# A fourth group of seven products in the down projection of the plain gated layers

## The chip, the cores and the metric

The kernel runs on one core of one Trainium2 chip. The metric is the device time of one execution in microseconds (us). Before the change the median of three runs was 2737.45 us (2737.21 to 2740.82).

## The reference

Two transformer blocks run one after the other on x of 512 tokens by 1024 channels, in float32. The first has two layers, each with a gated feed-forward network, a mixer (two kinds of attention and a short convolution), a second gated network and a gated per-token embedding. The second block has one layer: another mixer, a gated network with a convolution over tokens on its gate, and an embedding. The change is about the four plain gated networks of the first block:

```python
h = rmsnorm(x, g_pre)
x = x + 0.5 * rmsnorm((silu(h @ w_gate) * (h @ w_up)) @ w_down, g_post)
```

w_gate and w_up are 1024 by 2816, w_down is 2816 by 1024, which the kernel takes as 22 rows of 128 for the down product. The gated network of the second block has 24 such rows and keeps its old code.

## The kernel before

Five engines each run an instruction list of their own, written out by hand in the order of the source, and meet only at semaphores. Activations lie with channels on the 128 partitions and tokens along the free dimension. An engine that waits holds everything behind it in its list.

A float32 product is made of three matmuls in a reduced float32 format (`trio`, L742 to L744): high part of the weight times high part of the activation, low times high, high times low. So each piece of weight is split before use. `split_high` (L583) copies it on ScalarE into a rounded tile WH, `split_low` (L588) subtracts on VectorE and writes the rest to WL. The pieces are units of 128 by 1024 elements, and four pairs of tiles go round: the split of a unit waits until TensorE has finished the unit four before it. Activations have high and low parts too (HH, HL, and HIDH_HIGH, HIDL_LOW for the hidden rows).

Most products of a gated network are computed in groups of seven in place of eight (`tensor_seven`): a block is cut in quarters, sums of quarters of the weights are multiplied by sums of quarters of the activations, and the results are combined. A group has seven products (0 to 6), each of 24 matmuls of 256 columns. They accumulate in three banks of PSUM called x, y and z, and between them ScalarE copies partial results out: p1 after product 0, q5 after 1, u2 after 2, c11 after 3, u3 after 4, c21 after 6 (`scalar_copy`, L1697). Product 2 waits for p1, 4 for u2, 5 for q5, 6 for u3. VectorE makes c22 (L2542) and c12 (L2548) of them. Of the weight quarters, five are loaded by SyncE's queue; GpSimd's queue adds a further quarter onto two of them by an accumulating DMA (`gpsimd_weight_sums`, L3453), and VectorE adds two more times (`vector_weight_sum`, L2527, called weight sum 2 and 6 after the product that uses it). A quarter's buffer is free for the next load when the low part of the last product that reads it is done, or when weight sum 6 has read it. There are six such buffers.

A plain network has n = 11 blocks of gate and up columns: groups 0 and 1 done directly, groups 2 to 10 in sevens. Then comes the down projection, where the changed code stands:

- early rows (`tensor_early_rows`): rows 8 to 15 directly for one half of the output channels, four units of two rows, each of 24 matmuls of 512 columns;
- group 11 (g = n) and group 12 (n + 1): rows 0 to 7 in sevens, one half of the output each. They use sums of hidden rows, `row_sum` 0 to 3 (L2590), with a high part on ScalarE (L1753) and a low part on VectorE (L2615);
- group 13 (n + 2): rows 8 to 15 in sevens for the other half. Its row sums (`late_sum`) are made early, parked in device memory and fetched back (`sync_park`, `sync_fetch`) when group 12 has used the first ones;
- the last rows (`tensor_last_rows`): rows 16 to 21 directly into all eight banks. The four banks of one half get the result of group 11 by additions of VectorE (`vector_add`), the other four are seeded by ScalarE from the sums of groups 12 and 13 (`scalar_seed`, L1761), since their banks serve the groups until then.

The order around the change is written out in `scalar_ffn`, `scalar_early_rows`, `scalar_down_seven` for ScalarE and `vector_ffn`, `vector_early_rows`, `vector_first_down_seven` and so on for VectorE; `sync_sums` places the parked sums in SyncE's queue of loads.

## Time and profile before

| | |
|---|---|
| runs, median of three | 2737.45 us |
| profiled execution, its own time | 2738.5 us |
| its span, first to last instruction | 2736.6 us |
| TensorE matmul busy | 2727.2 us |
| VectorE, ScalarE, GpSimd busy | 2058.6, 1623.5, 142.1 us |
| granted TensorE clock | 1.00 of 2.4 GHz |
| read from device memory | 364.87 MB |

Times in the views are microseconds from the start of the span. Matmuls overlap, so the cost of one is the distance between successive starts and not its duration. The same holds for ScalarE and VectorE, where an instruction starts about 0.1 us before the end that the trace gives for the one ahead of it.

### The profile page before, as it was taken

What the parts mean: (1) busy time and instruction counts of PE and PEld (TensorE: products, weight loads), DVE (VectorE), ACT (ScalarE), POOL (GpSimd) and SP (SyncE); (2) the same over time, 40 slices, a digit from 0 to 9 for tenths busy, and PEclk for the clock granted to TensorE, in tenths of its full rate; (3) what the DMA queues carried; (4) which work ended last, traced back from release to release, by engine and by line L of the source; (5) the groups of instructions that cost most, each with busy time, mean ns of one, the idle gap of its engine ahead of it and who ended that gap; (6) DMA issues with size and microseconds to landing.
All of it is one profiled execution on the core that took longest, in us unless ns stands there. A gap on an engine that the chain in (4) does not pass through costs nothing.

```text
span 2736.6 us, 46133 instructions
## 1 busy us (share of the span) xinstructions
PE 2727.2 (100%) x18546; PEld 2488.6 (91%) x18546; DVE 2058.6 (75%) x2754; ACT 1623.5 (59%) x2519; POOL 142.1 (5%) x160
## 2 busy tenths in 40 slices
PE   9999999999999999999999999999999999999999
PEld 8999987599999999999976799999987889999998
DVE  7778766767687787787757587787876746989968
ACT  6556644665566685565626565566754546666665
POOL 0000000000000000000000000000001100000000
PEclk9999999999999999999999999999999999999999
DMA  7776614037776327775331247765233323777651
GB/s 220 180 196 174 178 55 101 17 101 185 190 211 162 103 84 206 178 213 158 93 92 49 93 131 178 207 164 169 78 97 92 93 77 101 181 194 203 153 179 55
DMA packets 177139, 382.55 MB, mean 140 GB/s; under 512 B 35616, under 2 KB 80032, under 8 KB 176928
## 3 DMA queue, kind: packets, MB, share of 16 engines
q1 hardware_dynamic: 159216, 315.63, 37.1%
q0 software_dynamic: 17568, 63.97, 13.7%
q8 instruction: 148, 2.42, 0.4%
q14 instruction: 63, 0.52, 0.1%
q10 hardware_dynamic: 144, 0.00, 0.0%
HBM read 364.87 MB, written 12.58 MB: 138 GB/s over the span
## 4 chain that ended last, share of the span: by engine, by line
PE 99%; DVE 0%; DMA 0%; issue 0%; ACT 0%; SPq 0%; DVEq 0%
PE banks L742 31%; PE banks L743 31%; PE banks L744 31%; PE banks L1292 1%; PE banks L1314 1%; PE banks L1351 1%; PE banks L1303 1%; PE banks L1355 0%; PE banks L1341 0%; PE banks L781 0%; PE banks L1445 0%; DVE PT L3179 0%; PE banks L1274 0%; PE banks L1238 0%; DMA X<-in_x 0%
## 5 line engine op out<-in xcount | busy, mean ns | idle before, releaser
L742 PE MATMUL banks<-HH,WH 128*128 128x256 f32 (+1 forms) x3244 | 1015.8, 313 | 0.6 <-DVE HL L2284 0.4
L743 PE MATMUL banks<-HH,WL 128*128 128x256 f32 (+1 forms) x3244 | 1010.9, 312 | 0.0
L744 PE MATMUL banks<-HL,WH 128*128 128x256 f32 (+1 forms) x3244 | 1010.7, 312 | 0.0
L742 PEld LDWEIGHTS banks<-HH,WH 128*128 128x128 f32 x3244 | 619.1, 191 | 43.6 <-issue 8.3
L743 PEld LDWEIGHTS banks<-HH,WL 128*128 128x128 f32 x3244 | 619.2, 191 | 34.7 <-issue 1.0
L744 PEld LDWEIGHTS banks<-HL,WH 128*128 128x128 f32 x3244 | 619.1, 191 | 34.1
L588 DVE TENSOR_TENSOR WL<-raw,WH 128x1024 fp32r<-128x1024 f32 (+1 forms) x308 | 370.5, 1205 | 215.6 <-ACT WH L583 214.4
L583 ACT ACTIVATE WH<-raw 128x1024 fp32r<-128x1024 f32 (+1 forms) x308 | 319.3, 1040 | 291.7 <-DVE raw L2527 121.9
L742 PE MATMUL banks<-SH,WH 128*128 128x256 f32 x1472 | 416.7, 283 | 0.8 <-issue 0.8
L743 PE MATMUL banks<-SH,WL 128*128 128x256 f32 x1472 | 416.6, 283 | 0.0
L744 PE MATMUL banks<-SL,WH 128*128 128x256 f32 x1472 | 416.6, 283 | 0.0
L588 DVE TENSOR_TENSOR WL<-extra_raw,WH 128x1024 fp32r<-128x1024 f32 x216 | 264.1, 1223 | 126.4 <-ACT WH L583 126.4
L583 ACT ACTIVATE WH<-extra_raw 128x1024 fp32r<-128x1024 f32 x216 | 227.3, 1052 | 133.1 <-DVE extra_raw L2527 95.8
L742 PE MATMUL banks<-HIDH_HIGH,WH 128*128 128x256 f32 (+1 forms) x936 | 293.1, 313 | 0.4 <-issue 0.4
L743 PE MATMUL banks<-HIDH_HIGH,WL 128*128 128x256 f32 (+1 forms) x936 | 292.1, 312 | 0.0
L744 PE MATMUL banks<-HIDL_LOW,WH 128*128 128x256 f32 (+1 forms) x936 | 292.0, 312 | 0.0
L742 PEld LDWEIGHTS banks<-SH,WH 128*128 128x128 f32 x1472 | 282.6, 192 | 1.2 <-issue 1.2
L743 PEld LDWEIGHTS banks<-SH,WL 128*128 128x128 f32 x1472 | 282.6, 192 | 0.0
L744 PEld LDWEIGHTS banks<-SL,WH 128*128 128x128 f32 x1472 | 282.6, 192 | 0.0
L588 DVE TENSOR_TENSOR WL<-spare_raw,WH 128x1024 fp32r<-128x1024 f32 (+2 forms) x141 | 170.6, 1210 | 73.4 <-ACT WH L583 72.8
L1697 ACT ACTIVATE C<-banks 128x512 f32<-128x512 f32 x224 | 132.5, 592 | 138.7 <-PE banks L744 136.4
L583 ACT ACTIVATE WH<-spare_raw 128x1024 fp32r<-128x1024 f32 (+2 forms) x141 | 146.1, 1036 | 94.5 <-PE banks L744 55.9
(341 smaller groups left out, 3666.8 us busy)
## 6 DMA issues: line engine op xcount, KB each, us to landing
extra_raw<-in_w_quarters SPq DMA_DIRECT2D x96, 512.0 KB, 4.3
raw<-in_w_quarters SPq DMA_DIRECT2D x48, 512.0 KB, 4.8
raw<-in_w_in SPq DMA_DIRECT2D x46, 512.0 KB, 3.7
spare_raw<-in_w_quarters SPq DMA_DIRECT2D x36, 512.0 KB, 4.1
extra_raw<-in_w_quarters POOLq DMA_DIRECT2D x36, 512.0 KB, 7.4
raw<-in_w_down SPq DMA_DIRECT2D x30, 512.0 KB, 3.7
extra_raw<-in_last_quarters SPq DMA_DIRECT2D x26, 512.0 KB, 4.3
raw<-in_w_quarters POOLq DMA_DIRECT2D x24, 512.0 KB, 6.0
```

What stands on the lines that cost most here:

```text
L583: e.activation(WH[tile_of[u]][:, 0:n], raw[raw_of(u)][:, 0:n], ACT.Copy).then_inc(*high.done((u,)))
L588: e.tensor_tensor(WL[tile_of[u]][:, 0:n], raw[raw_of(u)][:, 0:n], WH[tile_of[u]][:, 0:n].bitcast(F32), ALU.subtract).then_inc(*low.done((u,)))
L742: e.matmul(o, wh, ah, start=start, stop=False, skip_group_check=skip)
L743: e.matmul(o, wl, ah, start=False, stop=False, skip_group_check=skip)
L744: return e.matmul(o, wh, al, start=False, stop=stop, skip_group_check=skip)
L1292: e.matmul(ps[h][:, 0:w], QM[0:QK, 2 * q + h, i * P:w], KM[0:QK, 2 * q + h, 0:w], start=True, stop=False)
L1303: last = e.transpose(ps[2 + h][:, c], PB[t % 2 * 2 + h][:, c], ident)
L1314: last = e.matmul(target, vals[:, j, (head + h) * HD:(head + h + 1) * HD], source, start=j == 0, stop=j == TC - 1)
L1351: e.matmul(ps[4 + h][:, j * P:T], ntri, SP[:, h, j * P:T], start=False, stop=False, skip_group_check=True)
L1697: e.activation(target, third(bank), ACT.Copy).then_inc(*act.done((name, s, g)))
```

## The change

In the four plain networks (`four_down`), the early rows shrink from four units to one, rows 8 and 9. A fourth group, g = n + 3, takes rows 10 to 15 for the half that the early rows served, in seven products with three row pairs in place of four (`first = 1`), so of 18 matmuls each. It uses the same parked row sums as group 13 and weight quarters that were already laid out. The last rows begin with the seeded banks. ScalarE's and VectorE's lists are written anew for the stretch: high and low parts of rows 0 to 7 and of the row sums move further ahead or behind, those of rows 10 to 15 move into groups 11 to 13, and the seeds are interleaved with the fourth group's copies. The fetches of parked sums 2 and 3 move from the load of row 16 to loads of the fourth group's quarters.

```diff
+def four_down(s):
+    return s < 9
+def early_units(s):
+    return 1 if four_down(s) else 4
 def seven_groups(s):
-    return range(2, gated_groups(s) + 3)
+    return range(2, gated_groups(s) + 3 + four_down(s))
...
-                           *(((s, 11, "b11"), (s, 11, "b22")) if n > 11 else (W[s, "early", 0], W[s, "early", 2])))
+                           *(((s, 11, "b11"), (s, 11, "b22")) if n > 11 else (W[s, "early", 0], (s, 11, "sum"))))
...
-                if key == W[s, "down", DOWN_WHOLE]:
+                third, fourth = ((s, n + 3, "sum"), (s, n + 3, "b22")) if four_down(s) else (W[s, "down", DOWN_WHOLE],) * 2
+                if key == third:
                     sync_fetch(e, s, 2)
+                if key == fourth:
                     sync_fetch(e, s, 3)
...
-            late = g == gated_groups(s) + 2
+            late = g > gated_groups(s) + 1
+            first = 1 if g == gated_groups(s) + 3 else 0
...
-                    for kp in range(4):
+                    for kp in range(first, 4):
...
-                             early + late[2:] + late[:2], False)
+                             late + early if four_down(s) else early + late[2:] + late[:2], False)
...
-            for kp in range(4):
+            for kp in range(early_units(s)):
...
             if g == gated_groups(s) - 1:
-                return W[s, "early", i]
+                return W[s, "early", i] if i < early_units(s) else W[s, "seven", g + 1, i - 1]
...
                 if g == n - 1:
-                    scalar_hidden_high(e, s, 10)
-                    scalar_hidden_high(e, s, 11)
+                    for k in (0, 2) if four_down(s) else (10, 11):
+                        scalar_hidden_high(e, s, k)
...
+        def scalar_short_rows(e, s):
+            n = gated_groups(s)
+            scalar_c21(e, s, n - 1)
+            scalar_hidden_high(e, s, 4)
+            scalar_hidden_high(e, s, 6)
+            scalar_row_sum_high(e, s, 0)
+            split_high(e, W[s, "seven", n, 2])
+            scalar_row_sum_high(e, s, 1)
+            for k in range(1, DOWN_SEVEN, 2):
+                scalar_hidden_high(e, s, k)
...
+            if four_down(s) and g == n:
+                scalar_silu_half(e, s, n - 1, 1)
+                scalar_row_sum_high(e, s, 2)
             split_high(e, W[s, "seven", g, 4])
+            if four_down(s) and g == n:
+                scalar_row_sum_high(e, s, 3)
...
+            if four_down(s) and g == n:
+                for k in (10, 12, 14):
+                    scalar_hidden_high(e, s, k)
...
+        def scalar_last_down_seven(e, s, g):
+            x, y, z = seven_banks(s, g)
+            split_high(e, W[s, "seven", g, 3])
+            scalar_copy(e, s, g, "p1", 0, x, third(y), seven_free(s, g)[1][0])
+            split_high(e, W[s, "seven", g, 4])
+            scalar_seed(e, s, 0)
+            scalar_copy(e, s, g, "q5", 1, z, Q5C[:], vec.at("c22", s, g - 1))
+            split_high(e, W[s, "seven", g, 5])
+            scalar_copy(e, s, g, "u2", 2, x, place(s, g, 0, 1), vec.at("half_added", s, 0, 1))
+            split_high(e, W[s, "seven", g, 6])
+            scalar_copy(e, s, g, "c11", 3, y, place(s, g, 0, 0), act.at("seed", s, 0))
+            split_high(e, W[s, "down", DOWN_WHOLE])
+            scalar_hidden_high(e, s, DOWN_WHOLE)
+            scalar_copy(e, s, g, "u3", 4, x, place(s, g, 1, 1), vec.at("half_added", s, 1, 1))
+            scalar_seed(e, s, 1, act.at("c11", s, g))
+            split_high(e, W[s, "down", DOWN_WHOLE + 1])
+            scalar_seed(e, s, 2, vec.at("c12", s, g))
+            scalar_hidden_high(e, s, DOWN_WHOLE + 1)
+            scalar_copy(e, s, g, "c21", 6, x, place(s, g, 1, 0), act.at("seed", s, 1))
+            scalar_seed(e, s, 3, act.at("c21", s, g))
...
                 if g == n - 1:
                     vector_hidden_low(e, s, 8)
                     vector_hidden_low(e, s, 9)
+                    if four_down(s):
+                        vector_row_sum(e, s, 2)
                 split_low(e, after_seven(s, g, 1))
...
+        def vector_short_rows(e, s):
+            n = gated_groups(s)
+            vector_half_scale(e, s, n - 1, 1)
+            vector_weight_sum(e, s, n, 2)
+            vector_hidden_low(e, s, 4)
+            vector_hidden_low(e, s, 6)
+            split_low(e, W[s, "seven", n, 2])
+            vector_row_sum_low(e, s, 0)
+            vector_row_sum(e, s, 3)
+            vector_row_sum_low(e, s, 1)
+        def vector_first_of_four(e, s, g):
+            split_low(e, W[s, "seven", g, 3])
+            for k in range(1, DOWN_SEVEN, 2):
+                vector_hidden_low(e, s, k)
+            split_low(e, W[s, "seven", g, 4])
+            vector_half_hidden(e, s, g - 1, 1)
+            vector_row_sum_low(e, s, 2)
+            split_low(e, W[s, "seven", g, 5])
+            vector_row_sum_low(e, s, 3)
+            vector_weight_sum(e, s, g, 6)
+            split_low(e, W[s, "seven", g, 6])
...
+        def vector_third_of_four(e, s, g):
+            split_low(e, W[s, "seven", g, 3])
+            vector_hidden_low(e, s, 11)
+            vector_hidden_low(e, s, 13)
+            vector_hidden_low(e, s, 15)
+            split_low(e, W[s, "seven", g, 4])
+            vector_late_sum_low(e, s, 2)
+            split_low(e, W[s, "seven", g, 5])
+            vector_late_sum_low(e, s, 3)
+            vector_weight_sum(e, s, g, 6)
...
+        def vector_fourth_of_four(e, s, g):
+            vector_half_add(e, s, g - 1, 1, 0)
+            split_low(e, W[s, "seven", g, 3])
+            split_low(e, W[s, "seven", g, 4])
+            split_low(e, W[s, "seven", g, 5])
+            vector_weight_sum(e, s, g, 6)
+            split_low(e, W[s, "seven", g, 6])
+            split_low(e, W[s, "down", DOWN_WHOLE])
+            vector_hidden_low(e, s, DOWN_WHOLE)
+            vector_c22(e, s, g)
+            vector_add(e, s, g, 1, 1)
+            vector_c12(e, s, g)
+            vector_add(e, s, g, 0, 1)
+            vector_add(e, s, g, 0, 0)
+            split_low(e, W[s, "down", DOWN_WHOLE + 1])
+            vector_add(e, s, g, 1, 0)
+            vector_hidden_low(e, s, DOWN_WHOLE + 1)
```

## Rows read from the trace of the kernel before

**Rows 1.** The page: span, TensorE's busy time, granted clock in 40 slices.
```profile
span 2736.6 us, 46133 instructions
...
PE 2727.2 (100%) x18546; PEld 2488.6 (91%) x18546; DVE 2058.6 (75%) x2754; ACT 1623.5 (59%) x2519; POOL 142.1 (5%) x160
...
PEclk9999999999999999999999999999999999999999
```

**Rows 2.** Waits of TensorE: releaser, us in total, times, longest.
```profile
PE banks L742 <- issue: 1.2, 3, 0.6
```

**Rows 3.** Timeline of TensorE, first plain layer: start, duration, line, operation, tiles, shape.
```profile
231.82 0.40 PE L742 MATMUL banks<-HIDH_HIGH,WH 128*128 128x512 f32 x1
...
253.60 0.28 PE L742 MATMUL banks<-HIDH_HIGH,WH 128*128 128x256 f32 x1
...
273.76 0.28 PE L742 MATMUL banks<-HIDH_HIGH,WH 128*128 128x256 f32 x1
...
314.08 0.40 PE L742 MATMUL banks<-HIDH_HIGH,WH 128*128 128x512 f32 x1
```

**Rows 4.** VectorE's busy time, early rows to group 13: sum of four windows, one window.
```profile
253.58:273.74 20.16, 15.42 (x16) 1.00 0.48 131
...
sum 82.24, DVE 66.30; mean DVE 16.57
```

**Rows 5.** Timeline of VectorE in group 10, same layer.
```profile
220.34 1.22 DVE L2590 TENSOR_TENSOR HLF<-HLF,HIDF 128x1024 f32<-128x1024 f32 x1
221.47 1.22 DVE L2527 TENSOR_TENSOR extra_raw<-extra_raw,extra_raw 128x1024 f32<-128x1024 f32 x1
223.82 1.23 DVE L588 TENSOR_TENSOR WL<-extra_raw,WH 128x1024 fp32r<-128x1024 f32 x1 [1.12 <-ACT WH L583]
225.25 1.23 DVE L588 TENSOR_TENSOR WL<-raw,WH 128x1024 fp32r<-128x1024 f32 x1 [0.21 <-ACT WH L583]
226.40 1.29 DVE L2572 TENSOR_TENSOR HIDL_LOW<-HIDF,HIDH_HIGH 128x512 fp32r<-128x512 f32 x2
...
228.98 0.68 DVE L2542 TENSOR_TENSOR C<-Q5C,C 128x512 f32<-128x512 f32 x1
229.58 0.68 DVE L2548 TENSOR_TENSOR C<-banks,C 128x512 f32<-128x512 f32 x1
```

**Rows 6.** Timeline of ScalarE in group 10: split 6, c11, a split, u3.
```profile
222.73 1.06 ACT L583 ACTIVATE WH<-extra_raw 128x1024 fp32r<-128x1024 f32 x1 [0.59 <-DVE extra_raw L2527]
223.69 0.58 ACT L1697 ACTIVATE C<-banks 128x512 f32<-128x512 f32 x1
224.17 1.05 ACT L583 ACTIVATE WH<-raw 128x1024 fp32r<-128x1024 f32 x1
226.26 0.60 ACT L1697 ACTIVATE C<-banks 128x512 f32<-128x512 f32 x1 [1.04 <-PE banks L744]
```

**Rows 7.** DMA issues in the down groups: count, KB, median us to landing (last: one issue).
```profile
extra_raw<-in_w_down_quarters POOLq DMA_DIRECT2D x3, 512.0 KB, 5.4
raw<-in_w_down_quarters SPq DMA_DIRECT2D x5, 512.0 KB, 4.6
extra_raw<-in_w_down_quarters SPq DMA_DIRECT2D x4, 512.0 KB, 4.8
spare_raw<-in_w_down_quarters SPq DMA_DIRECT2D x3, 512.0 KB, 5.1
...
raw<-in_w_down_quarters POOLq DMA_DIRECT2D x1, 512.0 KB, 8.1
```

**Rows 8.** Timeline of the last layer's third down group: ScalarE, then TensorE.
```profile
2615.92 1.06 ACT L583 ACTIVATE WH<-extra_raw 128x1024 fp32r<-128x1024 f32 x1 [3.11 <-DMA extra_raw<-in_last_down_quarters]
...
2620.21 0.58 ACT L1697 ACTIVATE R<-banks 128x512 f32<-128x512 f32 x1
...
2620.55 0.28 PE L744 MATMUL banks<-HIDL_LOW,WH 128*128 128x256 f32 x1
2620.89 0.36 PE L742 MATMUL banks<-HH,WH 128*128 128x256 f32 x1
```

**Rows 9.** Timeline of ScalarE: the four seeds of the first plain layer.
```profile
314.56 2.16 ACT L1761 ACTIVATE banks<-C 128x512 f32<-128x512 f32 x4 [3.46 <-DVE C L2837]
```

More of the change, by code:

```diff
@@ L500, in place @@
         def place(s, g, t, m):
-            return two((R, RP)[t]) if g == gated_groups(s) + 2 else quadrant(t, m)
+            n = gated_groups(s)
+            if g < n + 2:
+                return quadrant(t, m)
+            return two((R, RP)[t]) if m else C[:, t, 0, :].rearrange("p (c t) -> p c t", c=2)
         def quarter_out(s, g, t, m):
@@ L561, in tiles_free @@
             if s is not None and STAGES[s] == "ffn":
-                e.wait_ge(*pe.at("unit", W[s, "seven", seven_groups(s)[-1 - (tile_of[u] == NSPLIT + 1)], 6]))
+                g = gated_groups(s) + 1 if tile_of[u] == NSPLIT + 1 else seven_groups(s)[-1]
+                e.wait_ge(*pe.at("unit", W[s, "seven", g, 6]))
             elif s is not None and STAGES[s] == "mix":
@@ L986, in seven_free @@
                 return group_free(s, g - 2 if g < n else n - 1)[:3]
-            first = [vec.at("evacuated", s, (n - 1) % 2, 3)] if g == n + 1 else [act.at("c21", s, n)]
-            return [first, [act.at("c11", s, g - 1)], [vec.at("c12", s, g - 1)]]
+            first = [vec.at("evacuated", s, (n - 1) % 2, 3)] if g == n + 1 else [act.at("c21", s, g - 2)]
+            second = [vec.at("half_added", s, 0, 0)] if g == n + 3 else [act.at("c11", s, g - 1)]
+            return [first, second, [vec.at("c12", s, g - 1)]]
         def row_sums(tile, i):
@@ L1033, in tensor_seven @@
                         last = trio(e, ps[bank][:, part(up)], high_of(u)[:, c], low_of(u)[:, c], *operand(kp),
-                                    opens and up == kp == 0, kp == 3, not (opens and up == 0))
+                                    opens and up == 0 and kp == first, kp == 3, not (opens and up == 0))
                 last.then_inc(*pe.done(("seven", s, g, ph), ("unit", u)))
@@ L1051, in tensor_ffn @@
             tensor_early_rows(e, s)
-            for g in seven_groups(s)[-3:]:
+            for g in down_groups(s):
                 tensor_seven(e, s, g)
-            added = [[vec.at("quarter_added", s, t, m) for t in range(2)] for m in range(2)]
+            last = n_groups + 3 if four_down(s) else n_groups
+            added = [[vec.at("quarter_added", s, last, t, m) for t in range(2)] for m in range(2)]
             early, late = (list(range(4 * half, 4 * half + 4)) for half in (n_groups % 2, 1 - n_groups % 2))
@@ L1753, in scalar_row_sum_high, with scalar_seed @@
             e.activation(row_sums(HH, i), row_sums(HLF, i), ACT.Copy).then_inc(*act.done(("row_sum_high", s, i)))
-        def scalar_seed(e, s, i):
+        def scalar_seed(e, s, i, *waits):
             n = gated_groups(s)
@@ L1759, in scalar_seed @@
                 e.wait_ge(*vec.at("half_added", s, t, i // 2))
-            e.wait_ge(*act.at("c21", s, n + 1))
+            for wait in waits:
+                e.wait_ge(*wait)
             e.activation(ps[group_banks(n - 1)[i]][:], C[:, i % 2, i // 2, :], ACT.Copy).then_inc(*act.done(("seed", s, i)))
@@ L1839, in scalar_ffn @@
                     scalar_silu_half(e, s, g, 0)
-            scalar_early_rows(e, s)
-            scalar_down_seven(e, s, n)
-            scalar_down_seven(e, s, n + 1)
-            scalar_down_seven(e, s, n + 2)
+            if four_down(s):
+                scalar_short_rows(e, s)
+            else:
+                scalar_early_rows(e, s)
+            for g in range(n, n + 3):
+                scalar_down_seven(e, s, g)
+            if four_down(s):
+                scalar_last_down_seven(e, s, n + 3)
             for k in range(DOWN_WHOLE + 2, 2 * n):
@@ L1919, in scalar_down_seven @@
                 scalar_late_sum_high(e, s, 1)
-            if g < n + 2:
+                if four_down(s):
+                    for k in (11, 13, 15):
+                        scalar_hidden_high(e, s, k)
+            if four_down(s) or g < n + 2:
                 split_high(e, after_seven(s, g, 2))
@@ L2721, in vector_ffn @@
                 if g == n - 1:
-                    vector_hidden_low(e, s, 10)
-                    vector_hidden_low(e, s, 11)
+                    for k in (0, 2) if four_down(s) else (10, 11):
+                        vector_hidden_low(e, s, k)
                 split_low(e, after_seven(s, g, 2))
@@ L2802, in vector_add @@
                 e.wait_ge(*act.at("c21" if t else "c11", s, g))
-            e.tensor_tensor(rows, rows, quadrant(t, m), ALU.add).then_inc(*vec.done(("quarter_added", s, t, m)))
+            e.tensor_tensor(rows, rows, place(s, g, t, m), ALU.add).then_inc(*vec.done(("quarter_added", s, g, t, m)))
         def vector_second_down_seven(e, s, g):
             split_low(e, W[s, "seven", g, 3])
-            e.wait_ge(*pe.at("early", s, 3))
+            e.wait_ge(*pe.at("early", s, early_units(s) - 1))
             vector_add(e, s, g - 1, 0, 1)
@@ L2817, in vector_second_down_seven @@
             split_low(e, W[s, "seven", g + 1, 0])
+            if four_down(s):
+                for k in (10, 12, 14):
+                    vector_hidden_low(e, s, k)
             split_low(e, W[s, "seven", g + 1, 1])
```

78 lines of the change are left out of this document (48 added, 30 removed).

## The prediction

> **What bounds the kernel now.** I read the page's busy time first. TensorE is busy for 2727.2 of 2736.6 us at a granted clock of 1.00 in every slice [rows 1]. The list of waits on TensorE comes next: its largest entry is 1.2 us over the whole span, and the one for the changed stretch (205 to 340 us, the end of the first plain layer) is empty [rows 2]. So nothing waits there for a copy, a split or a transfer. A change can gain only by giving TensorE less to do, and can lose by making it wait. The third view is TensorE's timeline at the seams of that stretch [rows 3]. The 96 matmuls of 512 columns of the early rows begin at 231.82, the 168 of 256 columns of the first down group at 253.60, those of the second at 273.76. One of 512 columns costs 21.78 / 96 = 0.2269 us, one of 256 costs 20.16 / 168 = 0.120 us.
>
> **Matmuls removed and added.** Three of the four early units go: 3 x 24 = 72 matmuls of 512 columns, 72 x 0.2269 = 16.34 us. The fourth group has seven products of 2 x 3 x 3 = 18 matmuls of 256 columns: 126 x 0.120 = 15.12 us. That is 1.22 us less in a stage and 4.9 us less in the four plain stages (0.18%). It is also the most that the change can give, since no TensorE wait stands there to be removed. The saving of an eighth of the products is nearly eaten by the halves: two matmuls of 256 cost 13 ns more than one of 512.
>
> Beside the rows stands a rule. The Trainium skill (TensorE: Matmul & The Clock Gate, "Wait — 56ns, not 53.3ns?") gives back-to-back matmuls N / 2.4 GHz and about 2.5 ns, which would be 215.8 and 109.2 ns. By it 1.78 us would go in a stage and 7.1 us in all. The rows show 226.9 and 120 ns at a granted clock of 1.00, so here the measured fixed part is about 13 ns, and I keep 4.9.
>
> **Work added beside TensorE.** Four more splits (VectorE 1.14 us, ScalarE 0.96 each), two weight sums (1.14), and the fourth group's six copies (0.5) on ScalarE, its c22, c12 and four additions (0.60) on VectorE: 4.6 + 2.3 + 3.6 = 10.5 us on VectorE, about 7 us on ScalarE. Starts of successive instructions give these figures: long ones 220.34 to 221.47 and 225.25 to 226.40, short ones 228.98 to 229.58 [rows 5], splits and copies on ScalarE 222.73 to 223.69 to 224.17 [rows 6]. VectorE is idle for 82.24 - 66.30 = 15.9 us from the early rows to the end of the third group [rows 4]. It would keep some 5 us, but the idle time must lie in the right places. The two below are where I find it does not.
>
> **The first group starts 16.3 us sooner, its preparation does not.** Group 11 begins at 231.82 + 24 x 0.2269 = 237.27, its product 6 at 237.27 + 6 x 2.88 = 254.55. VectorE's order is unchanged up to the low part of the first early unit at 225.25 [rows 5]. From there to weight sum 6 of group 11 its new order holds 14 long instructions (seven splits: early and products 0 to 5; row_sum 2 and 3; four row_sum_low; weight sum 2) and 16 short ones (ten low parts of rows, c22, c12, two scalings, two hidden halves). 14 x 1.14 + 16 x 0.60 + 0.1 = 25.7 us, with nothing to wait for by my count of ScalarE's order (its split for product 2 is ready just when VectorE is): the sum starts at 250.9. On the way row_sum_low 0 ends at 240.0 for a product that starts at 240.15, without reserve.
> Then ScalarE goes in order: split 6 starts 1.26 us after that sum (221.47 to 222.73), c11 0.96 later, the split for the next group's product 0 0.48 later, u3 0.96 later and 0.6 long [rows 5, 6]. u3 ends at 255.2 and TensorE, which resumes 0.10 us after such a copy (2620.21 + 0.58 to 2620.89) [rows 8], at 255.3: 0.7 us late. In group 10 of before, u3 waited for TensorE alone and had 2.1 us to spare (226.26 + 0.60, for a product at 231.82 - 2.88 = 228.94) [rows 3, 6]. Behind split 6 on ScalarE stand c11, the split of the next group and u3; none can pass it. Bounds: 0 (two VectorE instructions less than I count) to 1.5 us; I take 0.7, 2.8 us in all.
>
> **The fourth group needs its last quarter sooner.** Its products last 2.16 us (18 matmuls). Call its start T. The quarter for product 4 ("third") can load only when weight sum 6 of group 13 frees its buffer. From split 0 of group 13 on VectorE has 11 long and 8 short instructions to that sum without a gap, 17.3 us, and 1.2 for itself; that split comes 13.3 to 14.5 us after the start of group 12 (c11 there waits for product 3, 11.5 + 0.2, and split 0 and its low part follow 1.6 later; or up to 1.2 later if group 12's own accumulating DMA is slow). Two groups are 40.3 us, so the sum ends at T - 8.5 to T - 7.3; I take T - 7.9. The load takes 4.6 to 5.1 us, the accumulating DMA behind it 5.4 to 8.1 [rows 7], and I allow 0.3 for the hand-over: it lands at T + 1.8 to T + 6.2, and with 4.8 and a middling 6.2 at T + 3.4. From there runs a chain on ScalarE and VectorE: split 4, seed 0, q5, split 5 (starting 2.0 us after the landing), its low part and weight sum 6 (4.2), split 6 (5.5), c11, split of row 16, its high part, u3 (ends 9.0); then seed 1, split 17, c12 on VectorE, seed 2, high 17, c21 and seed 3, which ends at 14.0. A seed counts 0.52 (2.16 for four) [rows 9]. TensorE needs u3 at T + 12.96 and seed 3, after seven products and three banks of 0.68, at T + 17.16. So a landing up to T + 3.1 costs nothing, and each later one its excess: 0 to 3.1 us; I take 0.4, near the middling duration, 1.6 us in all. That such a chain reaches TensorE, the last layer shows: there ScalarE stood 3.11 us for the accumulating DMA, u2 came late behind it, and TensorE started at 2620.89 in place of 2620.67 [rows 8].
>
> **Edits at nothing.** The fetches of parked sums 2 and 3 make SyncE wait for products 4 and 5 of group 12 (some 25 us before the fourth group uses the quarters queued behind them). The park moved one place is issued long before row sum 0. The hidden high and low parts of rows 10 to 15 lie in groups 11 to 13, where VectorE waited for ScalarE. The new order of the last rows (seeded banks first) takes away the 2.7 us that covered four seeds after the third group; seeds 0 and 1 now lie inside the fourth group, and the price of the others is in the chain above. The last layer takes the old branches.
>
> **Sum.** -4.9 + 2.8 + 1.6 = -0.5 us. The profiled execution took 2738.5 us around its span of 2736.6; the median of the runs is 2737.45, 1.05 below it, and I put the difference on the median: 2737.0 us. Less than 0.2% (5.5 us) can't be told from no change here.
>
> **Rivals.**
> - All covers hold: 2737.45 - 4.9 = 2732.6 us. For it: VectorE's 15.9 us idle [rows 4] and the empty list of waits. Against it: 0.7 us missing at one named place.
> - Slower, by one mechanism: the accumulating DMA of the fourth group's third quarter comes at the late end, T + 6.2, and each stage waits 3.1 us there beside the 0.7: 4 x 3.8 - 4.9 = +10.3, 2747.8 us. It decides from a landing at T + 5.0 (0.7 + 1.9 > 1.2 + 1.4). For it: one such DMA of 8.1 us [rows 7] and the last layer's wait [rows 8]; against it: others took 5.4.
> - A matmul of 256 columns costs half of one of 512 in the new mix, 0.1135 us: 16.34 - 126 x 0.1135 = 2.04 us in a stage, 8.2 in all, 2729.3 us without a wait. Against it: 168 in a row at 0.120 [rows 3]. The Trainium skill's page on TensorE named above comes close to that half (109.2 to 215.8 ns).
> - The group runs, but out of step: the shorter early stretch makes each of seven products wait some 0.35 us for its split, 2.4 us a stage: 2737.45 - 4.9 + 9.8 = 2742.3 us. For it: product 1's row_sum_low has no reserve; against it: later groups have 1 to 2 us.
>
> **Chances.** Forecast 0.58 (own range 2734.5 to 2740.5), all covers hold 0.18, late DMA 0.12, out of step 0.10, the half price 0.02. The range 2732.5 to 2744 leaves out the most of the late DMA and the last rival. Faster by over 0.2% would need more than the 4.9 us there are: 0.03. Slower by over 0.2% is the late DMA and a small part of out of step: 0.14. Within: 0.83.
>
> **What would show it.** In the changed profile: 72 matmuls fewer of 512 columns and 126 more of 256 in each plain stage, still at 0.227 and 0.120; a wait of TensorE of 0.5 to 0.9 us ahead of group 11's product 6, with VectorE without a gap for some 25 us before; waits of 0 to 1 us ahead of the fourth group's product 6 or at the third seeded bank; the third quarter's split on ScalarE ended by the DMA. I am wrong if TensorE's busy time falls by other than about 5 us, if no wait stands at product 6, or if a wait over 2 us stands at a place that I priced at nothing.

## The result, and the profile after

Over four runs the changed kernel took 2748.19 us (2747.29 to 2751.16) and the kernel before, on the same chip, 2737.33: a ratio of 1.0038 [1.0026, 1.0051]. It is slower by 10.9 us (0.4%). Three single executions in the sets of the experiments below ran slow, one each of third14_kept (5786.87 us), small_add (14119.54) and the kernel before (2798.52); the ratios leave them out, and without them the first two medians are 2740.1 and 2740.5. The forecast, 2737.0 us, and its range missed it; the rival with the late DMA (2747.8 us) came near the time, though its sum is made up differently. Page of the profiled execution (2751.16 us), against [rows 1]:

```profile
span 2749.4 us, 46737 instructions
...
PE 2726.6 (99%) x18762; PEld 2494.8 (91%) x18762; DVE 2099.7 (76%) x2802; ACT 1647.0 (60%) x2559; POOL 149.4 (5%) x168
...
PEclk9999999999999999999999999999999999999999
```

TensorE has 216 instructions more, which is 4 x (126 - 72), the clock is full, and its busy time is even 0.6 us lower; yet the span grew by 12.8 us. So the time went into waits that the kernel before did not have [rows 2]. TensorE's waits in the changed kernel (releaser, us in total, times, longest):

```profile
PE banks L760 <- ACT RP L1718: 3.7, 4, 1.0
PE banks L760 <- ACT banks L1783: 2.7, 4, 0.7
PE banks L760 <- issue: 2.0, 3, 1.2
PE banks L760 <- DVE WL L604: 1.9, 3, 0.9
PE banks L760 <- ACT C L1718: 1.7, 4, 0.4
PE banks L760 <- DVE WL L2391: 1.2, 1, 1.2
```

Four times each, one per plain stage: u3 of the fourth group (RP), the last seed (banks), u3 of group 11 (C). The three of line 604 and part of "issue" are product 4 of groups 13 and 14. The entry of line 2391 stands at the start of the program. TensorE's timeline shows where in the first stage (against [rows 3]):

```profile
232.92 0.40 PE L760 MATMUL banks<-HIDH_HIGH,WH 128*128 128x512 f32 x1
...
238.39 0.28 PE L760 MATMUL banks<-HIDH_HIGH,WH 128*128 128x256 f32 x1
...
255.77 0.28 PE L762 MATMUL banks<-HL,WH 128*128 128x256 f32 x1
256.48 0.36 PE L760 MATMUL banks<-HIDH_HIGH,WH 128*128 128x256 f32 x1 [0.43 <-ACT C L1718]
...
299.91 0.28 PE L760 MATMUL banks<-HIDH_HIGH,WH 128*128 128x256 f32 x1
...
308.43 0.28 PE L762 MATMUL banks<-HIDL_LOW,WH 128*128 128x256 f32 x1
309.91 0.36 PE L760 MATMUL banks<-HH,WH 128*128 128x256 f32 x1 [1.20 <-issue]
...
315.42 0.36 PE L760 MATMUL banks<-HIDH_HIGH,WH 128*128 128x256 f32 x1 [0.96 <-ACT RP L1718]
...
320.55 0.50 PE L760 MATMUL banks<-HIDH_HIGH,WH 128*128 128x512 f32 x1 [0.67 <-ACT banks L1783]
```

256.48 is product 6 of group 11. The fourth group starts at T = 299.91; its products 4 (309.91) and 6 (315.42) and row 16's tenth matmul (320.55) wait. A bracket leaves out what the modelled end of the matmul before covers, so I count **lost time** from starts: each start less the one before, less 0.2267 us after a matmul of 512 columns or 0.120 after one of 256, every excess over 25 ns, from the early unit to row 17. Over the four plain stages:

| place | lost us by stage | sum | in the forecast |
|---|---|---|---|
| group 11, products 1 and 4 | 0.25, 0.25, 0.50, 0.25 | 1.2 | 0 |
| group 11, product 6 | 0.66, 0.67, 0.67, 0.67 | 2.7 | 2.8 |
| group 13, product 4 | 0.18, 0.63, 1.13, 0.81 | 2.7 | 0 |
| fourth group and row 16 | 3.57, 2.08, 2.18, 2.04 | 9.9 | 1.6 |
| all | 4.65, 3.62, 4.51, 3.76 | 16.5 | 4.4 |

16.5 less the 4.9 of the matmuls, less 0.9 that the last layer lost in the profiled execution before (at 2620.89 [rows 8] and row 16) and not in this one, is +10.7. The two spans differ by 12.8: this execution also began its first early row 1.1 us later (232.92 against 231.82), behind the wait at the start, and took 0.9 us longer after TensorE's last matmul had started (4.5 us against 3.7), which makes 12.7. The medians differ by 10.9: the profiled execution was 3.0 us above its median, and 2.0 of that are these two ends. So by estimate some 1 us of the 16.5 is not in the median. ScalarE in the first stage:

```profile
255.75 0.59 ACT L1718 ACTIVATE C<-banks 128x512 f32<-128x512 f32 x1
...
286.24 1.06 ACT L599 ACTIVATE WH<-extra_raw 128x1024 fp32r<-128x1024 f32 x1 [2.99 <-DMA extra_raw<-in_w_down_quarters]
...
306.31 1.06 ACT L599 ACTIVATE WH<-extra_raw 128x1024 fp32r<-128x1024 f32 x1 [2.90 <-DMA extra_raw<-in_w_down_quarters]
...
314.70 0.58 ACT L1718 ACTIVATE RP<-banks 128x512 f32<-128x512 f32 x1
...
319.89 0.60 ACT L1783 ACTIVATE banks<-C 128x512 f32<-128x512 f32 x1
```

The five quarters of a group are called b11, sum, b22, b21 and third, in the order of their loads; GpSimd adds onto sum and third. Twice ScalarE stands for an accumulating DMA into a "third" quarter: for group 13 until 286.24, for the fourth until 306.31. The copy at 314.70 and the seed at 319.89 release TensorE 0.14 and 0.06 us after they end. The second DMA: its issue on GpSimd, then the load and the addition by the table of issues (count, KB, us to landing):

```profile
298.85 0.86 POOL L3598 DMA_DIRECT2D extra_raw<-in_w_down_quarters  x1 [15.88 <-DMA extra_raw<-in_w_down_quarters]
```

```profile
extra_raw<-in_w_down_quarters SPq DMA_DIRECT2D x1, 512.0 KB, 5.1
extra_raw<-in_w_down_quarters POOLq DMA_DIRECT2D x1, 512.0 KB, 7.4
```

It lands at 306.3, T + 6.4; in the other stages at T + 4.9, 5.0 and 4.8.

The first of the two DMAs also delays the second. VectorE's low part of that quarter waits for ScalarE's split, and weight sum 6 of group 13, which frees the buffer for the fourth group's third quarter, stands behind it:

```profile
287.33 1.23 DVE L604 TENSOR_TENSOR WL<-extra_raw,WH 128x1024 fp32r<-128x1024 f32 x1 [1.28 <-ACT WH L599]
...
291.99 1.22 DVE L2593 TENSOR_TENSOR raw<-raw,extra_raw 128x1024 f32<-128x1024 f32 x1
```

The sum ends 7.0 us after group 13's third quarter lands, and T comes 13.7 us after that landing, in every stage; so the sum ends at T - 6.7.

The stretch ahead of group 13 is crowded. Windows of 20 us, of before and of after, at the same place counted from group 13's start (columns: window and length, busy time of PE, PEld, DVE, ACT and POOL, clock, DMA share, GB/s):

```profile
276.30:296.30 20.00, 20.00 (x169) 20.00 (x168) 15.29 (x17) 12.42 (x15) 1.25 (x2) 1.00 0.81 224
```

```profile
262.00:282.00 20.00, 20.00 (x169) 20.00 (x169) 17.79 (x21) 14.38 (x19) 1.76 (x2) 1.00 0.96 288
```

The DMA issues of the same windows, before and after, the four fetches:

```profile
HLF<-parked_sums SPq DMA_DIRECT2D x4, 512.0 KB, 4.1
```

```profile
HLF<-parked_sums SPq DMA_DIRECT2D x4, 512.0 KB, 6.6
```

The DMA engines are busy for 96% in place of 81%, and a fetch takes 6.6 us in place of 4.1. SyncE's issues of the last two fetches, before (group 13 starts at 293.92) and after (at 279.59):

```profile
288.40 3.40 SPq L672 DMA_DIRECT2D HLF<-parked_sums  x2
```

```profile
274.07 0.53 SPq L688 DMA_DIRECT2D HLF<-parked_sums  x1
274.64 0.62 SPq L651 DMA_DIRECT2D spare_raw<-in_w_down_quarters  x1
276.95 0.53 SPq L688 DMA_DIRECT2D HLF<-parked_sums  x1
```

They go out 5.5 and 2.6 us ahead of group 13 in both kernels, under their new keys too. New are the fourth group's first loads (274.64 is its sum quarter, its b11 goes out at 273.02), which now stand around them. Group 13's third quarter lands 6.6 to 7.6 us after group 13 starts; in the kernel before it was 2.0 to 5.4 us.

### The profile page after: what moved, and what is told of

It is laid out like the page before. It is cut to its first block, busy times and chain, and to the rows that moved or that the text cites. A ratio compares the mean times of both kernels' runs of the same rounds, so it can differ in the third digit from the quotient of the medians.

```text
span 2749.4 us, 46737 instructions
## 1 busy us (share of the span) xinstructions
PE 2726.6 (99%) x18762; PEld 2494.8 (91%) x18762; DVE 2099.7 (76%) x2802; ACT 1647.0 (60%) x2559; POOL 149.4 (5%) x168
## 4 chain that ended last, share of the span: by engine, by line
PE 72%; issue 14%; DMA 7%; DVE 4%; ACT 1%; SPq 1%; POOL 0%; ACTq 0%; POOLq 0%; DVEq 0%
PE banks L760 22%; PE banks L761 22%; PE banks L762 22%; DMA extra_raw<-in_w_down_quarters 4%; DMA extra_raw<-in_w_quarters 2%; PE banks L1313 1%; DVE WL L604 1%; PE banks L1335 1%; PE banks L1372 1%; ACT WH L599 1%; DMA raw<-in_w_quarters 1%; DMA raw<-in_w_down_quarters 1%; DMA spare_raw<-in_w_quarters 1%; PE banks L1324 1%; DVE HIDL_LOW L2638 0%
## 5 line engine op out<-in xcount | busy, mean ns | idle before, releaser
L760 PE MATMUL banks<-HH,WH 128*128 128x256 f32 (+2 forms) x3340 | 1043.5, 312 | 5.4 <-DVE WL L604 1.9
L761 PE MATMUL banks<-HH,WL 128*128 128x256 f32 (+2 forms) x3340 | 1037.7, 311 | 0.0
L762 PE MATMUL banks<-HL,WH 128*128 128x256 f32 (+2 forms) x3340 | 1037.4, 311 | 0.0
L760 PEld LDWEIGHTS banks<-HH,WH 128*128 128x128 f32 x3340 | 637.0, 191 | 49.7 <-issue 10.0
L761 PEld LDWEIGHTS banks<-HH,WL 128*128 128x128 f32 x3340 | 637.2, 191 | 34.6 <-issue 1.0
L762 PEld LDWEIGHTS banks<-HL,WH 128*128 128x128 f32 x3340 | 637.2, 191 | 34.2
L604 DVE TENSOR_TENSOR WL<-raw,WH 128x1024 fp32r<-128x1024 f32 x316 | 380.1, 1206 | 201.2 <-ACT WH L599 200.7
L599 ACT ACTIVATE WH<-raw 128x1024 fp32r<-128x1024 f32 x316 | 327.5, 1040 | 309.1 <-DVE raw L2593 146.9
L761 PE MATMUL banks<-HIDH_HIGH,WL 128*128 128x256 f32 (+1 forms) x912 | 275.2, 302 | 0.0
L762 PE MATMUL banks<-HIDL_LOW,WH 128*128 128x256 f32 (+1 forms) x912 | 275.0, 302 | 0.0
```

The source lines that it names most:

```text
L599: e.activation(WH[tile_of[u]][:, 0:n], raw[raw_of(u)][:, 0:n], ACT.Copy).then_inc(*high.done((u,)))
L604: e.tensor_tensor(WL[tile_of[u]][:, 0:n], raw[raw_of(u)][:, 0:n], WH[tile_of[u]][:, 0:n].bitcast(F32), ALU.subtract).then_inc(*low.done((u,)))
L760: e.matmul(o, wh, ah, start=start, stop=False, skip_group_check=skip)
L761: e.matmul(o, wl, ah, start=False, stop=False, skip_group_check=skip)
L762: return e.matmul(o, wh, al, start=False, stop=stop, skip_group_check=skip)
```

## The experiments

Theory: the fourth group's third quarter lands late, as the last of its five, and the short products can't cover it; group 13's waits have the same cause in the crowd. Rivals: ScalarE's and VectorE's chains are too long in any case, or the transfers share one stream so that an earlier place helps nothing. The kernel before, run beside each set, had medians from 2737.33 to 2738.25 us. "Lost" is the time defined above. The span less the lost time is 2730.4 to 2731.8 us in every experiment, so what differs between them is lost at these places.

| kernel | expected us | median us | ratio to before, 95% | lost us |
|---|---|---|---|---|
| changed |  | 2748.19 | 1.0038 [1.0026, 1.0051] | 16.5 |
| third14 | 2737 to 2740 | 2762.26 | 1.0090 [1.0076, 1.0104] | 28.7 |
| third1314 | 2734.5 to 2737.5 | 2766.67 | 1.0106 [1.0092, 1.0119] | 32.8 |
| u3first | 2745 to 2746.6 | 2747.10 | 1.0034 [1.0022, 1.0047] | 16.2 |
| all_fixed | 2732 to 2734 | 2767.74 | 1.0107 [1.0092, 1.0123] | 35.4 |
| third14_kept | 2737 to 2740 | 2740.25 | 1.0007 [0.9998, 1.0016] | 6.5 |
| third1314_kept | 2734.5 to 2738 | 2738.49 | 1.0000 [0.9992, 1.0009] | 4.8 |
| thirds_u3_kept | 2732.5 to 2736.5 | 2736.68 | 0.9993 [0.9984, 1.0002] | 4.6 |
| all_kept | 2731.5 to 2735.5 | 2736.28 | 0.9992 [0.9983, 1.0001] | 3.7 |
| covered | 2734.6 | 2734.66 | 0.9986 [0.9977, 0.9995] | 1.2 |
| small_add | 2737 to 2740.5 | 2740.63 | 1.0009 [0.9999, 1.0018] | 9.5 |
| small_loads | 2743.5 to 2746.5 | 2744.19 | 1.0023 [1.0014, 1.0033] | 11.9 |

Code is cut to the lines that differ. **third14** and **third1314** load the third quarter ahead of b22 and b21 (`+ 3`: the fourth group; `+ 2`: group 13 too):

```diff
-                for q in QUARTERS:
+                thirds_first = four_down(s) and name[2] >= gated_groups(s) + 3
+                for q in ("b11", "sum", "third", "b22", "b21") if thirds_first else QUARTERS:
```

> The changed kernel (2748.2 us), and in the fourth group the third quarter is loaded before b22 and b21, into the buffer that comes free some 6.5 us sooner. Theory late DMA: its accumulating DMA then lands about T - 0.5 in place of T + 4.9 to T + 6.4, the waits at the fourth group's products 4 and 6 and at the last seed (3.6 us in the first stage, 2.1 in the others, 9.9 in all) go: 2738.3 us, 2737 to 2740. Rival overload (VectorE and ScalarE have more work per product of 2.16 us than fits, the DMA only happens to be the last): the chain stays late by most of it, 2745 to 2748 us.

> As the one before, and in group 13 too the third quarter is loaded before b22 and b21. Theory late DMA: the waits at group 13's product 4 (0.2, 0.6, 1.1, 0.8 us in the four stages, 2.7 in all) go beside the 9.9: 2735.6 us, 2734.5 to 2737.5. Rival crowding (too many transfers at once between groups 12 and 13, in whatever order): third comes sooner but b22 or b21 later, so the 2.7 us stay or move: 2737.5 to 2741 us. Rival overload: over 2744 us.

Both were slower. In third14 the fourth group's waits all but went (0.2 us left a stage), and a greater one came at product 4 of group 13. SyncE, ScalarE, TensorE, and then the clock by windows (clock, DMA share and GB/s come last):

```profile
273.10 0.62 SPq L652 DMA_DIRECT2D spare_raw<-in_w_down_quarters  x1
286.14 0.33 SPq L652 DMA_DIRECT2D extra_raw<-in_w_down_quarters  x1
286.56 0.53 SPq L689 DMA_DIRECT2D HLF<-parked_sums  x1
...
291.45 1.06 ACT L1997 ACTIVATE HH<-HLF 128x1024 fp32r<-128x1024 f32 x1 [4.22 <-DMA HLF<-parked_sums]
292.42 0.58 ACT L1719 ACTIVATE R<-banks 128x512 f32<-128x512 f32 x1
...
289.45 0.28 PE L763 MATMUL banks<-HIDL_LOW,WH 128*128 128x256 f32 x1
293.10 0.55 PE L761 MATMUL banks<-HH,WH 128*128 128x256 f32 x1 [3.37 <-issue]
293.44 0.41 PE L762 MATMUL banks<-HH,WL 128*128 128x256 f32 x1
```

```profile
293.10:298.40 5.30, 5.30 (x25) 5.30 (x26) 4.18 (x5) 2.01 (x2) 0.00 (x0) 0.50 0.75 176
299.00:304.00 5.00, 5.00 (x44) 5.00 (x43) 3.80 (x5) 1.25 (x3) 0.00 (x0) 1.00 0.51 196
```

The fourth fetch hangs on the key of the quarter b22, which now stands behind a load that waits for its buffer until 286.14; in the changed kernel the fetch went out at 276.95. ScalarE needs it for a row sum and stands 4.22 us, u2 (R) comes behind it, TensorE starts 3.5 us late and then issues 25 matmuls at 0.213 us before the clock is back. So my own edit moved a second thing, and these two runs don't decide between the theories.

**u3first** (ScalarE; c11 stays where it was in the list, and both splits go behind u3, so that it too comes ahead of them):

```diff
-            split_high(e, W[s, "seven", g, 6])
+            copies_first = four_down(s) and g == n
+            if not copies_first:
+                split_high(e, W[s, "seven", g, 6])
...
             scalar_copy(e, s, g, "u3", 4, x, place(s, g, 1, 1), *u3_free)
+            if copies_first:
+                split_high(e, W[s, "seven", g, 6])
+                split_high(e, after_seven(s, g, 0))
```

> The changed kernel, and in group 11 ScalarE makes c11 and u3 ahead of the splits for product 6 and for the next group's product 0. Theory queue order (u3 is late because it stands behind a split that waits for VectorE): the wait of 0.66 us at group 11's product 6 goes but for some 0.1, in four stages 2.2 to 2.7 us: 2745.8 us, 2745 to 2746.6. Rival VectorE (the low part of product 6's weights is as late as u3): nothing to 0.8 us gained, 2747.4 to 2748.2.

Product 6 of group 11 lost 0.28 us a stage in place of 0.67, 1.6 us in all: the copy had stood behind the split. The time lies between the ranges of theory and rival, and its 1.1 us below the changed kernel are less than the intervals can tell apart. Product 4 of group 13 lost 0.97, 2.24, 0.70 and 0 us, 3.9 against 2.7. Counted from the first early row, its third quarter landed 0.4 and 1.2 us later than in the changed kernel in the first two stages, and 0.9 and 1.2 us sooner in the others; why stays open.

**all_fixed** joins both to two moves on VectorE:

```diff
-            split_low(e, W[s, "seven", n, 2])
             vector_row_sum_low(e, s, 0)
+            split_low(e, W[s, "seven", n, 2])
...
-            vector_half_hidden(e, s, g - 1, 1)
             vector_row_sum_low(e, s, 2)
+            vector_half_hidden(e, s, g - 1, 1)
```

> The edits of the two kernels before, and on VectorE row_sum_low 0 ahead of product 2's low split and row_sum_low 2 ahead of a hidden half in group 11 (waits there of 0.19 to 0.44 and 0.06 us). Theory (16.5 us of named waits, each with its own cause, stand against 4.9 us of matmuls saved): 2748.2 - 16.5 = 2731.7, with something left over 2732 to 2734 us, so 0.1 to 0.2% under the kernel before the change. Rival overload: the waits move on to other products, over 2740 us.

It has the same fault as third1314 (TensorE 5.0 to 6.8 us late at product 4 of group 13), and is as slow. In the third stage it also lost 1.7 us at product 2 of group 13.

**The four kept kernels** leave the fetches at their old places, by new keys (groups 13 and 14; third14_kept has only the last line), and add the edits above one by one:

```diff
-                if key == (s, n + 2, "b22"):
+                if key == (s, n + 2, "third" if four_down(s) else "b22"):
-                if key == (s, n + 2, "b21"):
+                if key == (s, n + 2, "b22" if four_down(s) else "b21"):
-                third, fourth = ((s, n + 3, "sum"), (s, n + 3, "b22")) if four_down(s) else (W[s, "down", DOWN_WHOLE],) * 2
+                third, fourth = ((s, n + 3, "sum"), (s, n + 3, "third")) if four_down(s) else (W[s, "down", DOWN_WHOLE],) * 2
```

> The changed kernel with the fourth group's quarters loaded in the order b11, sum, third, b22, b21, and the fetch of the fourth parked sum left where it stood in SyncE's queue (right behind the load of the sum quarter, ahead of the next load): its key is now the third quarter. Theory (the third quarter of the fourth group lands late, and the run of the same order without the kept fetch was slow because the fetch stood behind a load that waits for the low part of product 4 of group 13): the fetch is issued near 276 us in the first such stage as in the changed kernel, no matmul runs at the half clock, the waits at products 4 and 6 of group 14 and at row 16's tenth matmul (9.9 us over the four stages) go, and those of group 13 (2.7 us) and group 11 (2.7 us) stay: 2748.2 - 9.9 = 2738.3 us (2737 to 2740). Rival A (the new order of the loads itself is the harm of that run, the fetch only its first sign): product 4 of group 13 is again 3.5 to 5 us late in each stage, and the time is 2755 to 2762 us. Rival B (the addition takes as long as the traffic around it lets it, and an earlier place only moves the wait to the quarters behind it): 2743 to 2748 us.

> The same order of quarters in groups 13 and 14, with all four fetches left at their old places in SyncE's queue. Theory: the third quarter of group 13 is loaded some 2.9 us sooner, its addition lands before product 4 needs it, and the 2.7 us of waits at product 4 of group 13 go as well: 2748.2 - 9.9 - 2.7 = 2735.6 us (2734.5 to 2738). Rival (the loads, fetches and additions of this stretch share one stream, and the quarters pushed back are late in its place): no better than 2738.3 us, waits at products 3 or 5 of group 13.

> The same with ScalarE's copies of c11 and u3 of group 11 ahead of its two splits. Theory: product 6 of group 11 starts 0.5 us sooner in each of four stages (0.67 us late in the changed kernel, 0.18 in the run with that edit alone): 2735.6 - 2.0 = 2733.6 us (2732.5 to 2736.5). Rival (what starts sooner here waits longer at product 4 of group 13, as in the run with that edit alone, which gained about 1 us of 2): 2734.5 to 2735.6 us.

> The same with VectorE's low part of row sum 0 ahead of the low part of product 2 of group 11, and that of row sum 2 ahead of the last half of the hidden layer. Theory: the waits at products 1 and 4 of group 11 (0.25 us in three stages, 0.50 in one) go as well, and of the 16.6 us lost in the changed kernel about 1 us is left: 2733.6 - 1.2 = 2732.4 us (2731.5 to 2735.5), which is 5 us below the kernel before: the 288 products saved, and nothing given back. Rival (the fourth group can't be had without a wait, since the same transfers must land within the same stretch): 2736 us or more, no faster than the kernel before.

third14_kept in the first stage (SyncE, GpSimd, TensorE):

```profile
275.26 0.53 SPq L689 DMA_DIRECT2D HLF<-parked_sums  x1
286.41 4.98 SPq L652 DMA_DIRECT2D extra_raw<-in_w_down_quarters  x3
...
290.58 0.86 POOL L3599 DMA_DIRECT2D extra_raw<-in_w_down_quarters  x1 [10.02 <-DMA extra_raw<-in_w_down_quarters]
...
289.42 0.28 PE L761 MATMUL banks<-HH,WH 128*128 128x256 f32 x1
```

The fetch is back at 275.26, TensorE goes into product 4 of group 13 at 289.42 without a gap, and 22 us of third14 are gone: one key in a queue. Counted from T, the addition is issued 6.4 us sooner than in the changed kernel (290.58 at T = 298.06, 298.85 at 299.91; 4.5 to 5.6 us in the other stages). It takes 7.9 to 10.1 us in place of 6.6 to 7.7, as the second rival would have it, yet it lands at T + 0.4 to T + 2.6, and the fourth group and row 16 lose 0.2 to 1.1 us a stage in place of 2.0 to 3.6. Lost time was as expected (6.5 us, 6.65 by the sum), in another make-up: the fourth group kept 2.1 us, and group 13 lost 0.1 in place of 2.7, its third quarter having landed 0.5 to 1.8 us sooner without being moved; why stays open. The median lies 2 us above the expected 2738.3, though the lost time agrees: the profiled execution (2739.11) was one of the fastest, and the 16.5 us taken off came from an execution 3.0 us above its median. third1314_kept lost 1.7 us less and was 1.8 us faster; group 13 lost nothing. Its time is the rival's (no better than 2738.3), but the waits that the rival names, at products 3 or 5 of group 13, did not come. thirds_u3_kept was 1.8 us faster again: product 6 of group 11 lost 1.6 us less (in the profiled execution products 0 and 1 lost 1.2 more). all_kept removes the waits at products 1 and 4, but product 6 of group 11 (1.6 us) and row 16 (1.4 us) keep theirs, behind weight sum 6 and the last seed, so 2736.28 us in place of 2732.4, which can't be told from the kernel before; by the number the rival (2736 or more) came out here. All four lie 0.2 to 0.8 us above their ranges, and the intervals of one and the next overlap; those of the changed kernel and of any of the four do not.

**covered** moves these too:

```diff
             vector_row_sum_low(e, s, 2)
-            vector_half_hidden(e, s, g - 1, 1)
             split_low(e, W[s, "seven", g, 5])
             vector_row_sum_low(e, s, 3)
             vector_weight_sum(e, s, g, 6)
+            vector_half_hidden(e, s, g - 1, 1)
...
-            vector_add(e, s, g, 1, 1)
             vector_c12(e, s, g)
+            vector_add(e, s, g, 1, 1)
...
-            scalar_hidden_high(e, s, DOWN_WHOLE + 1)
             scalar_copy(e, s, g, "c21", 6, x, place(s, g, 1, 0), act.at("seed", s, 1))
             scalar_seed(e, s, 3, act.at("c21", s, g))
+            scalar_hidden_high(e, s, DOWN_WHOLE + 1)
```

and on ScalarE split 6 of group 11 goes ahead of u3 again, while the next group's split stays behind u3.

> The kernel all_kept with three more moves: in group 11 ScalarE does c11, split 6, u3 and then the next group's split, and VectorE does the weight sum 6 ahead of the last half of the hidden layer; in the fourth group VectorE does c12 ahead of an addition, and ScalarE does the last seed ahead of row 17's high part. Theory: of the 3.7 us that TensorE still lost in the four stages of all_kept, 1.6 us stood at product 6 of group 11 (0.28 to 0.54 a stage, behind the weight sum's split) and 1.4 us at row 16's tenth matmul (0.22 to 0.50 a stage, behind the last seed); about 1.1 and 0.6 of these go: 2736.3 - 1.7 = 2734.6 us, the interval of the ratio to the kernel before below 1. Rival (u3 or a low part is late in their place): 2736 us or more.

2734.66 us, as expected, and faster than the kernel before with the interval below 1. TensorE's waits on data of these stages shrink to two entries, both in the first stage (product 6 of the fourth group, and the thirteenth matmul of row 16); the other three lose nothing. In the first stage the addition took 9.9 us and landed at T + 4.3, 1.2 us behind the predicted break-even, and 1.2 us were lost; in the others it landed at T + 1.1 to T + 2.7:

```profile
PE banks L761 <- DVE banks L2912: 0.4, 1, 0.4
...
PE banks L761 <- ACT RP L1719: 0.3, 1, 0.3
```

**small_add** and **small_loads** measure the disputed cost without moving anything in a list: they leave out fifteen sixteenths of a transfer.

```diff
+                    cut = 64 if q == "third" and g == gated_groups(s) + 3 else UNIT
+                    target, source = raw_quarter(s, g, q)[:], W.quarter(s, g, other)
+                    if cut < UNIT:
+                        target, source = target[:, :cut], source[:, :cut]
+                    e.dma_start(target, source, accum_op=ALU.add).then_inc(*added[q].done((s, g)))
```

> The changed kernel with the accumulating DMA of the fourth group's third quarter cut from 1024 columns to 64: it leaves out fifteen sixteenths of that addition, and nothing is moved, in order or in queue. Theory (the fourth group waits only for this DMA's landing, which took 6.6 to 7.7 us in the changed kernel): at some 2 to 3 us it lands at about T + 0.5 in place of T + 4.8 to T + 6.4, ahead of the T + 3.1 from which it would decide, and the waits at product 4, product 6 and row 16's tenth matmul (9.9 us in all) go, while those of groups 11 and 13 (5.5 us) stay: 2748.2 - 9.9 = 2738.3 us (2737 to 2740.5). Rival (the chain of splits, copies and seeds on ScalarE and VectorE is too long for the seven short products in any case): product 6 and row 16's tenth matmul still wait about 1 us each in every stage, and the time is 2744 us or more.

```profile
extra_raw<-in_w_down_quarters POOLq DMA_DIRECT2D x1, 32.0 KB, 3.8
```

Even 32 KB take 3.5 to 4.0 us, but the landing comes to T + 0.8 to 1.9, and of the fourth group's 9.9 us 1.7 are left, all at row 16. That settles the cause of the other 8.1: this landing. The rest is the rival's share, ScalarE's and VectorE's chain to the last seed, 0.2 to 0.6 us a stage, though the landing is ahead of the predicted break-even. The median is 2.3 us over the expected 2738.3; the lost time is 2.9 over the sum: those 1.7, 2.4 more at products 0 and 1 of group 11, 1.3 less at group 13 by its changing landings.

```diff
+                        few = four_down(s) and key in ((s, gated_groups(s) + 3, "b11"), (s, gated_groups(s) + 3, "sum"))
+                        cut = 64 if few else UNIT
+                        e.dma_start(raw[slot][:, :cut], source[:, :cut]).then_inc(*landed[slot].done((key,)))
```

> The changed kernel with the fourth group's first two loads (its b11 and sum quarters, issued 6.5 and 5 us ahead of group 13) cut from 1024 columns to 64: it leaves out fifteen sixteenths of both, and moves nothing in order or in queue. They are two of the twelve transfers of 512 KB that were issued in the 15 us ahead of group 13, and stand beside the load and the addition of group 13's third quarter. Theory (group 13's third quarter is late because so many transfers share the stretch: DMA engines 96% busy there, 74% in the kernel before): its load and addition together, 14.8 to 16 us from issue to landing in the changed kernel, shorten by 2 us or more, the landing comes to T13 + 5.5 or sooner in place of T13 + 6.6 to 7.6, and the 2.7 us of waits at product 4 of group 13 go: about 2745.5 us (2743.5 to 2746.5), the fourth group's own waits staying. Rival (those two transfers take as long however few others there are, as the addition of 64 columns still took 3.5 to 4 us): the landing stays at T13 + 6.5 or later and the time at 2747 to 2749 us.

```profile
extra_raw<-in_w_down_quarters POOLq DMA_DIRECT2D x1, 512.0 KB, 5.5
```

With two loads nearly gone, group 13's addition (8.1 us in this stage of the changed kernel) takes 5.5, 5.5, 7.4 and 5.5 us and lands 4.5 to 6.9 us after group 13's start (T13) in place of 6.6 to 7.6, and product 4 loses 0.5 us in all in place of 2.7. The time is in the expected range, but its interval overlaps that of the changed kernel, so this rests on the addition and the wait, not on the time. (The 74% of the expectation is of 262 to 282 us in the kernel before; at the same place in the layer it is the 81% shown.) The loads of that quarter didn't become shorter (7.1 to 9.1 us, 6.7 to 8.3 in the changed kernel), so the two loads explain the longer addition, not the whole lateness; what makes the load long stays open.

## Why the prediction was wrong

- **Matmuls: right.** The counts and the spacing (0.227 and 0.120 us) came as computed; 2736.6 - 4.9 - 0.9 = 2730.8, and every experiment's span less its lost time lies within 1.0 us of it. The rule of the Trainium skill for back-to-back matmuls (TensorE: Matmul & The Clock Gate, "Wait — 56ns, not 53.3ns?") would have put it 2.2 us lower.
- **Group 11, product 6: right** (0.7 taken, 0.66 to 0.67 measured, ended by u3 behind split 6). The row sum that I called "without reserve" did cost 0.19 to 0.44 us a stage, and I gave it no term.
- **The failed step: "it lands ... at T + 3.4".** Measured T + 6.4, 4.9, 5.0 and 4.8. The weight sum ended at T - 6.7 in every stage (taken T - 7.9, bounds T - 8.5 to T - 7.3), the load took 3.6 to 5.1 us (4.8), the addition 6.6 to 7.7 (6.2), the hand-over 0.4 to 0.5 (0.3). The mechanism held: each landing less the break-even of T + 3.1 makes 3.3, 1.8, 1.9 and 1.7 us, 8.7 in all, against 9.9. The sum was mis-sized in two terms. The weight sum was 1.2 us late in every stage because VectorE did not run "without a gap": it stood behind group 13's own late addition, for which I had no term. Where that addition lands 4 us or more sooner, in third1314_kept, the sum ended at T - 8.4 to T - 7.1, about as taken. And for the addition I took 6.2 us, between the 5.4 and the 8.1 of [rows 7], which had been measured with the queues at another load; the break-even was near, where every further 0.1 us costs 0.4. The chain to the last seed is longer than I added up: row 16 still lost 0.2 to 0.6 us a stage in small_add with the landing ahead of T + 3.1.
- **No term for group 13, which lost 2.7 us.** Under "edits at nothing" I looked at whom the fetches with new keys make wait. They go out at the same places as before; what I left out is that the fourth group's b11 and sum are loaded among them: ten transfers of 512 KB are issued in the 14 us ahead of group 13 (in the first stage of the profiled execution; the expectation of small_loads says twelve). The Trainium skill (DMA: Bandwidth & Descriptors, Issuing engines are not separate DMA queues) says that transfers from different engines run on the same DMA engines. The trace agrees: two of SyncE's loads nearly gone gave GpSimd's addition 1.9 to 3.3 us back in three stages of four (small_loads). My condition for being wrong, a wait over 2 us in a place priced at nothing, was met only over the stages together.
- **The late DMA rival** was the right mechanism at the fourth group, and its number near by some luck: it had 12.4 us at the fourth group (9.9 measured) and none at group 13 or products 1 and 4. Its chance of 0.12 was too low for a break-even inside the range of the landing.
- All covers hold (2732.6 us) is what the kernel named covered came within 2.1 us of, at 2734.66, after all these edits. The half price showed nowhere: 256 columns cost 0.120 us. Of out of step, only products 1 and 4 of group 11 showed (1.2 us, where it had 9.8); the other products that the table above doesn't name started on time.

## What to carry to other kernels

A group that makes TensorE's work shorter takes away cover from everything behind it: find the last transfer of its chain, and if the break-even lies inside that transfer's measured range, issue it sooner: here 4 to 6 us sooner did it, though the transfer itself then took longer. When loads are reordered, look at what else hangs on their keys in the same queue: one fetch left behind a waiting load cost 22 us here. Price a new load also by what it shares the DMA engines with at its place, and by the waits that this puts into the chain of the next group. With nearly all of that covered, the gain was 0.14% (0.05 to 0.23), where the matmuls could give 0.18%.

## What the runs showed of the hardware

An accumulating DMA of 512 KB from GpSimd's queue took 5.2 to 10.3 us in this stretch over all these kernels, and one of 32 KB still 3.5 to 4.0 us (small_add). After 3.37 us without a matmul (third14) TensorE's granted clock was 0.50, the 1.2 GHz level, for 25 matmuls (0.213 us each); after 2.00 us without one, in u3first, it stayed at 1.00. The fall and return added about 2.4 us to the wait of 3.5. Two rows of u3first, the wait and the window behind it:

```profile
878.23 0.35 PE L760 MATMUL banks<-HH,WH 128*128 128x256 f32 x1 [2.00 <-ACT R L1718]
...
878.20:884.00 5.80, 5.77 (x48) 5.80 (x49) 4.67 (x5) 3.44 (x4) 0.00 (x0) 1.00 0.75 214
```
